# Early input projections beside the gather: four places for high parts, results taken two groups later, four banks, and low parts on VectorE

## The reference, cut to what matters

```python
def chunk_fn(hc):                        # 128 tokens
    q = (hc @ w_query).reshape(TOKEN_CHUNK, PEER_HEADS, 2, PEER_HALF)
    sc = jnp.einsum('thpd,pnd->thpn', q, sub_keys)
    ...                                  # top 16 of each half, top 16 of the 256 pairs
    u = expert_u[expert_idx]             # 8 heads x 16 experts for each token
    act = jax.nn.gelu(jnp.einsum('thkd,td->thk', u, hc), approximate=False)
    vv = expert_v[expert_idx]
    return jnp.einsum('thk,thkd->td', gate * act, vv)
...
x = rmsnorm(x + peer_ffn(...), final_g)  # end of the first block
h = rms_norm(x, norm_g[l])               # begin of the second
p = h @ w_in[l]                          # 1024 -> 7552 columns
```

## Time and profile before

| what | value |
|---|---|
| median of 3 runs | 2598.53 us (2597.46 to 2606.31) |
| the profiled execution | 2591.51 us, span 2589.7 us |
| busy share of the span | PE 86%, DVE 68%, POOL 34%, ACT 33% |
| instructions | 34862 |
| granted clock of TensorE, mean | 0.95 |
| DMA | 710.39 MB, mean 274 GB/s |
| issues on the gather's line | 512, from 493.3 to 2031.1 us |

### The profile page before, as it was taken

How to read it: one execution, slowest core, us unless ns; L and a number is a source line. 1 busy time by engine, 2 the same in 40 slices (tenths; PEclk the granted TensorE clock), 3 DMA queues, 4 the chain that set the end, 5 groups by cost and what they waited for, 6 DMA issues and landing times. The chain is left out here.

```text
span 2589.7 us, 34862 instructions
## 1 busy us (share of the span) xinstructions
PE 2223.4 (86%) x12550; PEld 1488.6 (57%) x12550; DVE 1757.5 (68%) x3907; ACT 851.3 (33%) x1966; POOL 879.5 (34%) x649
## 2 busy tenths in 40 slices
PE   8998999988988998777778877677777898999999
PEld 7886667744444444232333333555566688876677
DVE  7998797676667666677776777656464537556753
ACT  4222762242323232232423243222221242224741
POOL 0001213444455445443335554354453300021133
PEclk9999999999999999999999999788888989998999
DMA  4332215799999999999999999677787664223142
GB/s 149 104 109 94 78 56 206 266 416 410 400 410 408 409 417 403 412 421 421 418 417 403 416 413 415 266 281 296 285 326 263 212 205 134 89 90 131 50 167 106
DMA packets 135482, 710.39 MB, mean 274 GB/s; under 512 B 14480, under 2 KB 23568, under 8 KB 69520
## 3 DMA queue, kind: packets, MB, share of 16 engines
q0 software_dynamic: 73728, 536.90, 51.5%
q1 hardware_dynamic: 61584, 171.26, 18.8%
HBM read 686.61 MB, written 21.50 MB: 273 GB/s over the span
## 5 line engine op out<-in xcount | busy, mean ns | idle before, releaser
L2133 PE MATMUL bank<-peer_uv,peer_diag 128*128 128x512 f32 x1856 | 896.6, 627 | 192.7 <-ACT peer_diag L1509 185.0
L1878 DVE SCALAR_TENSOR_TENSOR peer_uv<-peer_uv,h 128x1024 f32<-128x1024 f32 x512 | 649.8, 1280 | 306.4 <-DMA peer_uv<-in_peer_uv,peer_index 306.2
L1561 POOL DMA_INDIRECT peer_uv<-in_peer_uv,peer_index x512 | 552.2, 1079 | 822.1 <-PE bank L2133 698.2
L2133 PEld LDWEIGHTS bank<-peer_uv,peer_diag 128*128 128x128 f32 x1856 | 358.8, 200 | 627.8 <-issue 625.3
L165 PE MATMUL bank<-hT_high,weight_high 128*128 128x512 f32 (+1 forms) x952 | 427.6, 449 | 117.0 <-POOL weight_low L241 109.7
L216 ACT ACTIVATE weight_high<-weight_ring 128x1024 fp32r<-128x1024 f32 x171 | 180.8, 1057 | 580.0 <-PE bank L167 574.4
L167 PE MATMUL bank<-hT_high,weight_low 128*128 128x512 f32 (+1 forms) x952 | 364.9, 383 | 0.0
L166 PE MATMUL bank<-hT_low,weight_high 128*128 128x512 f32 (+1 forms) x952 | 364.6, 383 | 0.0
L233 POOL TENSOR_TENSOR weight_low<-weight_ring,weight_high 128x1024 fp32r<-128x1024 f32 x52 | 127.1, 2445 | 594.1 <-ACT weight_high L216 594.1
L165 PEld LDWEIGHTS bank<-hT_high,weight_high 128*128 128x128 f32 x952 | 192.8, 203 | 185.1 <-POOL weight_low L241 124.4
L241 POOL TENSOR_TENSOR weight_low<-weight_ring,weight_high 128x1024 fp32r<-128x1024 f32 x79 | 199.7, 2528 | 281.6 <-ACT weight_high L216 280.2
(11 more groups left out here) (462 smaller groups left out, 2904.6 us busy)
## 6 DMA issues: line engine op xcount, KB each, us to landing
weight_ring<-in_weights SPq DMA_DIRECT2D x218, 512.0 KB
z_store<-fill_stage SPq DMA_DIRECT2D x36, 256.0 KB, 2.4
peer_uv<-in_peer_uv,peer_index POOLq DMA_INDIRECT x512, 9.0
z_store<-early_stage SPq DMA_DIRECT2D x34, 192.0 KB
merge_z<-z_store SPq DMA_DIRECT2D x8, 768.0 KB, 6.5
merge_z<-z_store SPq DMA_DIRECT2D x12, 512.0 KB, 4.3
raw_query<-in_weights SPq DMA_DIRECT2D x10, 512.0 KB, 6.6
raw_out<-in_weights SPq DMA_DIRECT2D x8, 512.0 KB, 6.8
```

Of the source, the lines that this page charges most:

```text
L1561: pool.indirect_dma_start(uv[:, p % SLOTS], None, peer_uv, bass.IndirectOffsetOnAxis(index[:, n % 2, p % TOPK:p % TOPK + 1], 0)).then_inc( ...
L1878: nc.vector.scalar_tensor_tensor(uv[:, p % SLOTS, 0:D], uv[:, p % SLOTS, 0:D], 1.0, h2[:, t], ALU.mult, ALU.mult, accum_out=dots[:, p % TO ...
L2133: mm = nc.tensor.matmul(bank[2 * t + c][:], diag[:, p % SLOTS], uv[:, p % SLOTS, D + c * 512:D + (c + 1) * 512], start=(n == first_of(t) a ...
```

## The change

Seven edits in one:
- the early units have four places for high parts instead of two (`high_at`, two of them in room that the stage has left), from the first `rwkv` unit (`EARLY_FROM`) on;
- ACT takes the result of unit n in the slot of group `z_group(n) + 2` (`KEEP_BEHIND`), and makes the high part of unit n+4 right behind it; before it was the high part of n+2 first and then the result, in the slot of `z_group(n) + 1`;
- the results go through four PSUM banks (2 to 5) instead of two (4, 5), and PE waits for the copy of the unit four back;
- the low parts of all units from the third query unit on, 69 of them, are made by DVE between a group's dot products and its weights (`low_group` says in which group) instead of by POOL ahead of gathers;
- SP loads the next unit when PE has ended one, without waiting for the copy of its result;
- SP stores a result two rows later, behind that load;
- POOL keeps the two first low parts; its part behind the gather (`LOWS_BESIDE`) is empty now.

`HIGHS`, `KEEP_BEHIND` and `FIRST_LOW` are new; `LOWS_BESIDE` comes out as 71, which is all of them.

```diff
@@ -80,6 +80,7 @@
...
 TOTAL = sum(n for _, n in UNITS)
+EARLY_FROM = first_unit("rwkv")
 EARLY_T = T - P
@@ -209,11 +210,17 @@
...
+    def high_at(self, u):
+        if EARLY_FROM <= u < WHOLE[0]:
+            return self.early_high[(u - EARLY_FROM) % 4]
+        return self.high[:, split_index(u) % 2]
     def high_part(self, act, u, i=0):
...
             act.wait_ge(self.arrived[u % RING], 16 * i + 16 * (u // RING + 1))
-            self.nc.scalar.activation(self.high[:, split_index(u) % 2].bitcast(F32R), self.ring[:, u % RING], ACT.Copy
+            self.nc.scalar.activation(self.high_at(u).bitcast(F32R), self.ring[:, u % RING], ACT.Copy
                                       ).then_inc(self.high_ready, 1)
@@ -230,7 +237,7 @@
...
             pool.wait_ge(self.high_ready, RING * i + (split_index(u) + 1))
-            self.nc.gpsimd.tensor_tensor(self.low[:, slot].bitcast(F32R), self.ring[:, slot], self.high[:, split_index(u) % 2],
+            self.nc.gpsimd.tensor_tensor(self.low[:, slot].bitcast(F32R), self.ring[:, slot], self.high_at(u),
                                          ALU.subtract).then_inc(self.split, 1)
@@ -238,14 +245,14 @@
...
         eng.wait_ge(self.high_ready, split_index(u) + 1)
-        vector.tensor_tensor(self.low[:, u % RING].bitcast(F32R), self.ring[:, u % RING], self.high[:, split_index(u) % 2],
+        vector.tensor_tensor(self.low[:, u % RING].bitcast(F32R), self.ring[:, u % RING], self.high_at(u),
                              ALU.subtract).then_inc(self.split, 1)
-        self.lows = u + 1
+        self.lows = max(self.lows, u + 1)
...
         pe.wait_ge(self.split, RING * i + (split_index(u) + 1))
-        return Split(self.high[:, split_index(u) % 2], self.low[:, u % RING])
+        return Split(self.high_at(u), self.low[:, u % RING])
@@ -1120,6 +1127,26 @@
...
+HIGHS = 4
+KEEP_BEHIND = 2
+FIRST_LOW = 2
+def low_group(n):
+    if n < QUERIES + 2:
+        return query_group(n - 2) + 2
+    if n < QUERIES + DT + 2:
+        return mem_group(n - QUERIES - 2) + 1
+    e = n - QUERIES - DT
+    return Z_FROM + 1 + e - 2 if e < HIGHS else z_group(e - HIGHS) + 3
+LOWS_BESIDE = next(n for n in range(FIRST_LOW, QUERIES + DT + EARLY_UNITS + 1)
+                   if n == QUERIES + DT + EARLY_UNITS or low_group(n) > LAST_GROUP)
+assert all(low_group(n) < low_group(n + 1) for n in range(FIRST_LOW, LOWS_BESIDE - 1))
 def merge_and_experts(nc, w, bank, cols, const, ident, subkeys, z_store, attnT, h2T, peer_uv, x, gain, gain_row, mem, mem_store,
@@ -1157,6 +1184,8 @@
...
         last_h = same_place(nc, "last_h", [P, DT, P], w.high_offset + 4 * DT * P * ((WHOLE[0] + 1) % 2))
+        other = [same_place(nc, f"early_high{i}", [P, DT, P], attnT.high_offset + 4 * D * (i + 1)) for i in range(2)]
+        w.early_high = [w.high[:, EARLY_FROM % 2], w.high[:, (EARLY_FROM + 1) % 2], other[0][:], other[1][:]]
         early_stage = same_place(nc, "early_stage", [P, 2, EARLY_T], attnT.high_offset)
@@ -1279,12 +1308,21 @@
...
                 w.load(sp, r0 + Z_UNITS + RING)
+                def early_store_row(n):
+                    sp.wait_ge(z_kept, Z_UNITS + n + 1)
+                    sp.dma_start(early_store[n][:, 0:EARLY_T], early_stage[:, n % 2]).then_inc(early_stored[n % 2], 16)
                 for n in range(EARLY):
-                    sp.wait_ge(z_kept, Z_UNITS + n + 1)
+                    if n < EARLY - RING:
+                        w.load(sp, r0 + Z_UNITS + RING + n + 1)
+                    if n >= KEEP_BEHIND:
+                        early_store_row(n - KEEP_BEHIND)
                     if n == EARLY - RING:
...
                     w.load(sp, r0 + Z_UNITS + RING + n + 1)
-                    sp.dma_start(early_store[n][:, 0:EARLY_T], early_stage[:, n % 2]).then_inc(early_stored[n % 2], 16)
+                for n in range(EARLY - KEEP_BEHIND, EARLY):
+                    early_store_row(n)
                 sp.wait_ge(kv_stored, 16)
@@ -1467,7 +1505,7 @@
...
-                    w.finished(act, r0 + n)
+                    act.wait_ge(w.done, r0 + n + 1)
                     if n == 0:
@@ -1479,7 +1517,9 @@
...
                             act.wait_ge(early_stored[e % 2], 16 * (e // 2))
-                    nc.scalar.activation(to, bank[4 + n % 2][:, 0:EARLY_T], ACT.Copy).then_inc(z_kept, 1)
+                    nc.scalar.activation(to, bank[2 + n % 4][:, 0:EARLY_T], ACT.Copy).then_inc(z_kept, 1)
+                    if n + HIGHS < EARLY_UNITS:
+                        w.high_part(act, r0 + n + HIGHS)
@@ -1520,7 +1560,9 @@
...
                         next(memories)
-                    while zs < EARLY_UNITS - Z_AFTER and z_group(zs) < g:
+                    if g in (Z_FROM, Z_FROM + 1):
+                        w.high_part(act, r0 + 2 + g - Z_FROM)
+                    while zs < EARLY_UNITS - Z_AFTER and z_group(zs) + KEEP_BEHIND <= g:
                         keep_z(zs)
@@ -1541,14 +1583,7 @@
...
                 for g, n, q, t, h in groups():
-                    if lows < 2:
-                        if g >= 2:
-                            w.low_part(pool, nc.gpsimd, u0 + lows)
-                            lows += 1
-                    elif lows < QUERIES + 2 and query_group(lows - 2) + RINGS + 2 <= g or (
-                            QUERIES + 2 <= lows < QUERIES + DT + 2 and mem_group(lows - QUERIES - 2) + RINGS + 1 <= g) or (
-                            QUERIES + DT + 2 <= lows < QUERIES + DT + EARLY_UNITS and
-                            z_group(lows - QUERIES - DT - 2) + RINGS + 2 <= g):
+                    if lows < FIRST_LOW and g >= 2:
                         w.low_part(pool, nc.gpsimd, u0 + lows)
@@ -1561,7 +1596,8 @@
...
                                                 ).then_inc(arrived[g % RINGS] if g < LAST_GROUP else last_arrived[p % GROUP], 16)
-                for n in range(lows, QUERIES + DT + EARLY_UNITS):
+                pool.wait_ge(w.split, split_index(u0 + LOWS_BESIDE))
+                for n in range(LOWS_BESIDE, QUERIES + DT + EARLY_UNITS):
                     w.low_part(pool, nc.gpsimd, u0 + n)
@@ -1863,6 +1899,7 @@
...
                 dve.wait_ge(x_normed, 1)
+                lows = FIRST_LOW
                 for g, n, q, t, h in groups():
@@ -1879,6 +1916,11 @@
...
                             next(ahead, None)
+                    if lows < LOWS_BESIDE and low_group(lows) <= g:
+                        if lows == FIRST_LOW:
+                            dve.wait_ge(w.split, split_index(u0 + lows))
+                        w.low_part(dve, nc.vector, u0 + lows)
+                        lows += 1
                     if g == 0:
@@ -1904,6 +1946,7 @@
...
                         next(memories)
+                assert lows == LOWS_BESIDE
                 for _ in finish(TT - 1):
@@ -1945,10 +1988,10 @@
...
                         ring = w.wait(pe, r0 + n)
-                        if n >= 2:
-                            pe.wait_ge(z_kept, n - 1)
+                        if n >= 4:
+                            pe.wait_ge(z_kept, n - 3)
                         for k in range(DT):
-                            mm = product(nc, bank[4 + n % 2][:, 0:EARLY_T], ring[:, k], h3T[:, k, 0:EARLY_T], k == 0, k == DT - 1)
+                            mm = product(nc, bank[2 + n % 4][:, 0:EARLY_T], ring[:, k], h3T[:, k, 0:EARLY_T], k == 0, k == DT - 1)
                             if k == DT - 1:
...
                             yield
```

## The result

| | before | after |
|---|---|---|
| median of the compared runs | 2597.99 us | 2449.35 us (2445.02 to 2452.47) |
| ratio, 95% interval | | 0.9429 [0.9391, 0.9468] |
| the profiled execution, and its span | 2591.51, 2589.7 us | 2445.02, 2443.2 us |
| gather before the early units | 1116.2 us | 1108.7 us |
| early stage | 445.9 us | 316.9 us |

What follows compares the result with a forecast made beforehand. It took the early stage to be bound by a cycle of waits through PE's sums, POOL's gathers and low parts. 2591.5 - 98.0 + 1.0 = 2494.5, plus 7.0 to the median: 2501.5, predicted 2502 us, range 2470 to 2560.

Steps and rivals of the forecast that it cites:

- The period of 7.1 us: Early stage: a group takes 7.1 us, 49 groups 347.9 us instead of 445.9, so 98.0 us less.
- the fast place: Early stage before, 1741.4 to 1760.6 us: three groups in 19.2 us, 6.4 each, DMA share 0.98 at 390 GB/s.
- the DMA floor: Early stage: 127.1 MB for 49 groups makes transfers the limit, 6.3 us a group at 412 GB/s, 6.65 at 390.
- Rival 1: Early stage: landings wholly hidden, 6.4 us a group, 132.3 us less, 2467 us; chance 0.13.
- The store behind the load: Early stage: load, store landing (8.0 us), copy and low part form a 13.5 us chain, hidden within two groups.
- rival 2: Early stage: store and load become the new chain with 11.7 us landing, 8.4 us a group, 2565 us; chance 0.15.
- The 24 low parts of queries and memory: Full gather: moving them from POOL to DVE gives 0; up to 10 us less or 5 more.
- DVE's load: Early stage: 4.24 us a group without contention plus 1.22 for the low part, 5.5 us, so DVE has room.
- the two-port warning: POOL's gathers: DVE's two-port mode blocks descriptor writing, so gathers come late more often; 4 us a group at most, sum unchanged.
- PE's floor of a group: Early stage: eight steps of a unit and one pick's products take PE 5.38 us at full clock.
- PE at the low clock: Early stage: PE stays at 1.2 GHz, 9.8 us a group, 34.3 us more, 2634 us; chance 0.06.
- The end: After the gather: the last two stores both go out after the last unit's end, 1 us more (0 to 3).

Runs made afterwards that it cites:

- the run that turns the order round: Changed kernel with SP issuing the early store ahead of the next unit's load instead of behind it: 2448.57 us, beside 2450.41 for the changed kernel; early stage 310.0 against 317.2.
- the idle subtraction: Kernel before with all low parts on DVE, plus 24 unused POOL subtractions in the gather, one in every fourth group from 49 to 141: 2457.68 us, 0.9445.

## Why the prediction was wrong, point by point

- **The bound before** (a cycle over PE's sums, POOL's gathers, the low part and PE): right. Two edits that cut it at different places each freed more than 100 us.
- **The period of 7.1 us**: the step that failed. It was the 6.4 of the fast place, the 6.65 of the DMA floor at 390 GB/s, and half a microsecond "for landings and head changes". Measured: 6.47. Rival 1, the floor itself at 6.4 us, came true within 1%, and I had given it 0.13 because the fast place "emptied a backlog of loaded weights". The half microsecond came from no row. The half was added to the upper end of the floor, at 390 GB/s; the stage holds 399, without the late stores 408 to 410. This makes 347.9 - 316.9 = 31.0 us of the 52.
- **The store behind the load**: chain and landing were judged rightly as hidden for the most part. ACT stands 1.3 us a group, which the prediction named as the mark of rival 2; that mark was badly chosen, since ACT has two thirds of the stage idle. The cost is 7 us, by the run that turns the order round.
- **The 24 low parts of queries and memory, set at 0**, with "up to 10 us less": they gave 7.5 in the compared executions and about 11 over twelve. The 49.6 us that DVE stands for gathered rows seemed to cover everything. But a stage in which the DMA engines stand at 1.01 can still be 1% quicker (415 against 410 GB/s), and a share cannot show that.
- **DVE's load**: 5.5 us a group forecast, 258.0 / 49 = 5.27 measured. Weights 0.215 (0.21 forecast), row sums 1.277 (1.26), contention gone: right. The Trainium skill (SBUF — State Buffer, "SBUF: two separate sides") has a VectorE operation with two SBUF inputs and a GpSimd operation that reads SBUF take their shared port pair one at a time, each for its whole length. The dot product of 3.48 us beside POOL's 2.37, where it takes 1.22 alone, agrees: it ends 1.09 us after the subtraction, and 19 others of the gather before do so too (1.08 to 1.10 us). In four other places the dot product began 0.63 to 0.65 us earlier, kept its length, and the subtraction took 2.78 to 2.81 us in place of 2.35, as here:

```profile
1412.34 1.22 DVE L1878 SCALAR_TENSOR_TENSOR peer_uv<-peer_uv,h 128x1024 f32<-128x1024 f32 x1
1412.98 2.81 POOL L241 TENSOR_TENSOR weight_low<-weight_ring,weight_high 128x1024 fp32r<-128x1024 f32 x1
```

The recorded starts do not tell who goes first: the stretched dot product above began 0.02 us ahead of the subtraction, and the one beside the idle subtraction 0.65 us. That gathers would come late more often, which the working took from the two-port warning, has no row for it: nothing here shows that the moved subtraction runs in that mode.
- **PE's floor of a group** was misread: between 1613.56 and 1618.94 us there are seven steps and not eight, so that eight take 5.9 us and not 5.38. It changes nothing, as both are below the DMA floor; PE was busy 283.6 / 49 = 5.79 us a group.
- **PE at the low clock** did not come (0.98). **The end**, +1.0 forecast, +0.3 measured; both copies in it wait for a store, 2.26 and 2.95 us:

```profile
1928.44 0.49 ACT L1520 ACTIVATE early_stage<-bank 128x384 f32<-128x384 f32 x1 [2.26 <-DMA z_store<-early_stage]
1931.98 0.49 ACT L1520 ACTIVATE early_stage<-bank 128x384 f32<-128x384 f32 x1 [2.95 <-DMA z_store<-early_stage]
```

- **What no step spoke of**: 10.2 us in the rest of the program, within the spread of single executions, and 2.7 of the offset from execution to median (7.0 taken over from before, 4.3 after). The medians put the gain at 148 to 150 us in three groups of runs, and gather, early stage and end give 136 of it, 140 with the gather's 11. The 8 to 12 us between have no stage that shows them, as only one execution of the kernel before was profiled; whether the change has a part in them stays open.

The sum: 31.0 + 7.5 + 0.7 + 10.2 + 2.7 = 52.1 us; the miss is 2501.5 - 2449.35 = 52.15. Had the period been 6.47, the forecast would have been 2470 us, still 21 us above the measured time. The range was too narrow below: it ended at 2470, above the 2467 us of rival 1 itself, without the gain in the gather that the working allowed and without the 10 us by which the rest of the program differs from execution to execution. At its upper end it was the same: rival 2 had 2565, the range 2560.

## What to carry to other kernels

When a cycle of waits is cut and the transfers were already near a floor, put the forecast on the floor itself at the best rate that a neighbouring stage holds, and add only what a row shows; a safety margin belongs in the range. Two edits that cut the same cycle at different places do not add up: time each alone, since the cheaper one may be the whole gain, and the other may bring a wait of its own. A term that is hidden in a full stage is not free before the stage's rate with and without it has been compared.
